# mLSTM tail of a head: denominator and variance products placed one by one behind projection blocks

## What is computed

```
hN = _rmsnorm(x, norm_g[l]);  p = _split_in(hN @ w_in[l])
mq = silu(_causal_dwconv(p["m_q"], ...));  mk = silu(_causal_dwconv(p["m_k"], ...))
s   = einsum('bhld,bhsd->bhls', qc, kc) * exp(logD - m_t[..., None])
num = ... + einsum('bhls,bhse->bhle', s, vc)
den = ... + sum(s, axis=-1)
h   = num / maximum(abs(den), exp(-m_t))[..., None]
var = mean(square(h - mu), axis=-1)
hn  = (h - mu) * rsqrt(var + NORM_EPS)          # times mh_norm_g
ya  = sigmoid(p["m_o"]) * mh * silu(p["m_z"])
```

## Time and profile before

| | us |
|---|---|
| median of three runs | 1608.32 (1608.13 to 1611.36) |
| the profiled execution | 1609.1 |
| its span | 1607.3 |
| TensorE matmuls busy | 1533.4 (95% of the span) |
| VectorE, ScalarE, GpSimd busy | 759.3, 639.4, 684.8 |
| mean granted TensorE clock | 0.983 of full |

### The profile page before, as it was taken

One profiled execution on the slowest core, in us unless ns is written; L12 is line 12 of the kernel. 1 busy time (PEld: TensorE's weight loads), 2 busy tenths in 40 slices (PEclk: granted clock), 3 DMA queues, 4 the chain that ended last, 5 costly groups with the idle time before them and its releaser, 6 DMA issues.

```text
span 1607.3 us, 25456 instructions
## 1 busy us (share of the span) xinstructions
PE 1533.4 (95%) x10002; PEld 1226.4 (76%) x10002; DVE 759.3 (47%) x1767; ACT 639.4 (40%) x1345; POOL 684.8 (43%) x661
## 2 busy tenths in 40 slices
PE   5899999999899899999999899999999989999997
PEld 3777777677688788787877687878788867776887
DVE  4435555455543434534355454733433564455154
ACT  4234444445432533333334353434332344444331
POOL 2534344343432533443435444535255434444462
PEclk8999999999999999999999899999999999999999
DMA  9121111111023322322221322222121221111222
GB/s 395 39 77 42 39 54 53 53 53 54 27 80 105 105 73 79 110 82 80 85 100 53 105 86 79 80 70 88 53 101 57 79 105 53 53 53 53 79 83 75
DMA packets 23143, 128.23 MB, mean 80 GB/s; under 512 B 2417, under 2 KB 4593, under 8 KB 9073
## 3 DMA queue, kind: packets, MB, share of 16 engines
q1 hardware_dynamic: 22880, 126.35, 22.3%
q10 hardware_dynamic: 144, 0.26, 0.0%
HBM read 124.50 MB, written 2.10 MB: 79 GB/s over the span
## 4 chain that ended last, share of the span: by engine, by line
PE 82%; DVE 8%; ACT 3%; issue 3%; POOL 3%; DMA 1%; SPq 0%; POOLq 0%; DVEq 0%; ACTq 0%
PE PS L1516 16%; PE PS L1518 15%; PE PS L1517 15%; PE PS L1596 7%; PE PS L1631 6%; PE PS L1606 6%; PE PS L1509 3%; PE PS L1510 3%; PE PS L1511 3%; DVE sm L2209 2%; PE PS L1684 1%; PE PS L1676 1%; POOL WL L2536 1%; DMA XC<-in_xt 1%; PE PS L1529 1%
## 5 line engine op out<-in xcount | busy, mean ns | idle before, releaser
L2536 POOL TENSOR_TENSOR WL<-W,WH 128x512 fp32r<-128x512 f32 x304 | 400.4, 1332 | 326.7 <-ACT WH L1787 326.5
L1516 PE MATMUL PS<-HX,WH 128*128 128x512 f32 (+1 forms) x1008 | 412.8, 410 | 7.9 <-POOL WL L2536 3.7
L1518 PE MATMUL PS<-HX,WL 128*128 128x512 f32 (+1 forms) x1008 | 391.3, 388 | 0.0
L1517 PE MATMUL PS<-LX,WH 128*128 128x512 f32 (+1 forms) x1008 | 390.7, 388 | 0.0
L1516 PEld LDWEIGHTS PS<-HX,WH 128*128 128x128 f32 x1008 | 193.1, 192 | 54.5 <-issue 14.0
L1518 PEld LDWEIGHTS PS<-HX,WL 128*128 128x128 f32 x1008 | 191.7, 190 | 39.8
L1517 PEld LDWEIGHTS PS<-LX,WH 128*128 128x128 f32 x1008 | 192.7, 191 | 33.3 <-issue 2.6
L1787 ACT CAST WH<-W 128x512 fp32r<-128x512 f32 x320 | 186.9, 619 | 40.9 <-PE PS L1511 21.1
L1873 ACT ACTIVATE AR<-PS,sm 128x768 f32<-128x768 f32 (+4 forms) x160 | 115.5, 722 | 164.1 <-DVE sm L2214 93.7
L2209 DVE TENSOR_REDUCE sm<-PS 128x1 f32<-128x512 f32 (+4 forms) x224 | 150.0, 670 | 51.7 <-PE PS L1596 47.1
L2603 POOL TENSOR_SCALAR AR<-AR,sm 128x768 f32<-128x768 f32 (+1 forms) x96 | 74.8, 779 | 186.9 <-DVE sm L2225 186.9
(11 more groups left out here) (286 smaller groups left out, 2542.7 us busy)
## 6 DMA issues: line engine op xcount, KB each, us to landing
W<-in_wu SPq DMA_DIRECT2D x98, 1024.0 KB, 4.9
AR<-in_wu SPq DMA_DIRECT2D x8, 1024.0 KB, 10.8
AR<-in_biasb SPq DMA_DIRECT2D x32, 256.0 KB, 2.6
XX<-in_xt SPq DMA_DIRECT2D x2, 1024.0 KB, 6.0
XC<-in_xt SPq DMA_DIRECT2D x1, 1024.0 KB, 14.4
out<-XX SPq DMA_DIRECT2D x2, 512.0 KB, 4.1
out<-XX SPq DMA_DIRECT2D x4, 256.0 KB, 2.2
C<-in_cc SPq DMA_DIRECT2D x1, 770.5 KB, 8.4
```

The source lines that it names most:

```text
L1516: e.matmul(o, wh, xh, start=(k == 0), stop=False)
L1517: e.matmul(o, wh, xl, start=False, stop=False)
L1518: t = e.matmul(o, wl, xh, start=False, stop=(k == 7))
L2536: e.tensor_tensor(WL[:, d, a:z], W[:, n % 2, a:z], WH[:, d, a:z].bitcast(F32), ALU.subtract).then_inc(*s_wl_pool.by(n, q))
```

## The change

The two rows `m_den` and `m_var` are cut into single products, `m_den_part` (ten) and `m_var_part` (eight). The whole tail of a head becomes a generator, `m_tail`, and `with_tail` runs a projection and takes one step of the generator behind each of its blocks. It is used for the next head's `mq`, `mk` and `mv` (64 blocks in all), and for `nq` after the last head. Counted in blocks, the denominator's products stand behind blocks 1 to 10, the other engines' `m_den` and the first variance product behind block 11, the last variance product behind block 18, `m_var` of the other engines behind 19, `m_scale` behind 27 (the third block of the second half of `mk`), `parts_y` behind 43. The banks of the ring are taken at these places too. The table steps stay where they were.

```diff
+        def with_tail(g):
+            for _ in g:
+                next(tail[0], None)
...
-                run(pj(g, un, 0, T, 128 * m, "h", o))
+                with_tail(pj(g, un, 0, T, 128 * m, "h", o))
...
-            if later:
-                later.pop(0)()
...
+        def m_tail(hd):
+
             mps["den", hd] = bank(ONE.take(("mden", hd), (s_dsq, (hd,))))
+            for q in range(4):
+                for j in range(q + 1):
+                    do("m_den_part", hd, q, j)
+                    yield
             do("m_den", hd)
-
-        def m_var(hd):
             mps["var", hd] = bank(ONE.take(("mvar", hd), (s_vv, (hd,))))
+            for q in range(4):
+                for m in range(2):
+                    do("m_var_part", hd, q, m)
+                    yield
             do("m_var", hd)
+            for _ in range(8):
+                yield
+            m_scale(hd)
+            for _ in range(16):
+                yield
+            parts_y(hd)
...
-                run(pjt(("mv", hd, s), un, s, "h", o))
+                with_tail(pjt(("mv", hd, s), un, s, "h", o))
...
-            later[:] = [lambda hd=hd: m_den(hd), lambda hd=hd: m_var(hd), lambda hd=hd: m_scale(hd), lambda hd=hd: parts_y(hd)]
+            tail[0] = m_tail(hd)
...
-                run(pj(("nq", m), un, 0, T, 128 * (m % 2), "h", o))
+                with_tail(pj(("nq", m), un, 0, T, 128 * (m % 2), "h", o))
                 do("n_query", m)
                 do_later(3)
+                if m == 3:
+                    run(tail[0])
...
+            def m_den_part(hd, q, j):
+                if q == 0:
+                    free(w, ("mden", hd))
+                t = e.matmul(mps["den", hd][:, q:q + 1], E[j][:, 128 * q:128 * q + 128], c("ones", 0, 1), start=(j == 0), stop=(j == q))
+                if q == 3 and j == 3:
+                    t.then_inc(*s_den.by(hd))
+
+            def m_var_part(hd, q, m):
+                if q == 0 and m == 0:
+                    free(w, ("mvar", hd))
+                    w.wait_ge(*s_nsq(hd, 1))
+                t = e.matmul(mps["var", hd][:, q:q + 1], sqv[m][:, 128 * q:128 * q + 128], c("ones", 0, 1), start=(m == 0), stop=(m == 1))
+                if q == 3 and m == 1:
+                    t.then_inc(*s_vsum.by(hd))
```

More of the change, by code:

```diff
@@ L1185, in conv @@
             un.done(s_proj, *g)
-        later, tabs = [], list(range(1, 6))
+        tail, tabs = [iter(())], list(range(1, 6))
         do("table", 0)
@@ L1192, in do_later @@
                 do("table", tabs.pop(0))
-            if later:
-                later.pop(0)()
-        def m_den(hd):
+        def m_tail(hd):
             mps["den", hd] = bank(ONE.take(("mden", hd), (s_dsq, (hd,))))
+            for q in range(4):
+                for j in range(q + 1):
+                    do("m_den_part", hd, q, j)
+                    yield
             do("m_den", hd)
-        def m_var(hd):
             mps["var", hd] = bank(ONE.take(("mvar", hd), (s_vv, (hd,))))
+            for q in range(4):
+                for m in range(2):
+                    do("m_var_part", hd, q, m)
+                    yield
             do("m_var", hd)
+            for _ in range(8):
[4 more added lines that the diff above has]
+            parts_y(hd)
         def parts_y(hd):
@@ L1685, in m_num @@
                 t.then_inc(*s_hn.by(hd, m))
-            def m_den(hd):
-                free(w, ("mden", hd))
-                o = mps["den", hd]
-                for q in range(4):
-                    for j in range(q + 1):
-                        t = e.matmul(o[:, q:q + 1], E[j][:, 128 * q:128 * q + 128], c("ones", 0, 1), start=(j == 0), stop=(j == q))
-                t.then_inc(*s_den.by(hd))
-            def m_var(hd):
-                free(w, ("mvar", hd))
-                w.wait_ge(*s_nsq(hd, 1))
-                o = mps["var", hd]
-                for q in range(4):
-                    for m in range(2):
-                        t = e.matmul(o[:, q:q + 1], sqv[m][:, 128 * q:128 * q + 128], c("ones", 0, 1), start=(m == 0), stop=(m == 1))
-                t.then_inc(*s_vsum.by(hd))
+            def m_den_part(hd, q, j):
[11 more added lines that the diff above has]
+                    t.then_inc(*s_vsum.by(hd))
             def m_scale(hd):
@@ L1772, in tensor @@
                                score=score, turn=turn, pv=pv, m_gates=m_gates, m_gate_col=m_gate_col, m_exp=m_exp, m_qk=m_qk,
-                               m_num=m_num, m_den=m_den, m_var=m_var, m_scale=m_scale, n_rotate=n_rotate, n_hidden=n_hidden,
+                               m_num=m_num, m_den_part=m_den_part, m_var_part=m_var_part, m_scale=m_scale, n_rotate=n_rotate, n_hidden=n_hidden,
                                n_cmp_out=n_cmp_out, cmp=cmp, cmp_turn=cmp_turn, x_wb=x_wb))
```

## The result

| | before | after |
|---|---|---|
| median, four runs each | 1609.1 us (1608.13 to 1611.36) | 1624.64 us (1624.19 to 1627.87) |
| the profiled execution, its span | 1609.1, 1607.3 | 1624.86, 1623.1 |
| TensorE matmuls busy | 1533.4 | 1534.1 |
| mean granted TensorE clock | 0.983 | 0.982 |

The ratio after to before is 1.0105, with an interval of 1.0091 to 1.0119: slower by about 1%, 16 us. The forecast was 1617.3 us, in a range of 1608.5 to 1621: the direction was right, the size was half, and the range missed the time.

A forecast was written before the change was run, and what follows sets the result against it. TensorE's stream, busy all the time in the heads, was taken as the bound. Waits 11.3, removed drops -4.8, steady -0.3 and new drops +2.8 gave +9.0 us: span 1616.3, time 1617.3 us, range 1608.5 to 1621.

The forecast's parts named there:

- waits in the value projections (with the factor row's): TensorE waits for late value quarters and at the factor row: 3.3, 4.7 and 3.3 us in heads 1 to 3.
- clock drops in the query stretch, gone: Three half-clock stretches behind denominator rows disappear with single placing: 3 x 1.6 = 4.8 us less.
- pairs against rows: On TensorE, 18 pairs at 0.22 us replace rows of 4.04 us a head: 0.3 us less over four heads.
- new drops in the value projections: Half clock after head 2's wait and one other, about 1.4 us each: 2.8 us more.
- The chain on VectorE and GpSimd: Key convolution, `m_scale` multiplications, then value splits: quarter 2 ready at 30.8 us, quarter 3 at 32.1 from head start.
- The table step of head 2: Table load and sine on ScalarE delay the key's copy from 20.5 to 22.0: 1.4 us more wait.
- rival (d): Weight loads of pairs hide behind blocks: one of two, 1609.4 us, chance 0.04; both, 1601.5 us, chance 0.03.
- rival (a): Same value-projection waits, but no clock drop behind them: 1614.5 us; chance 0.17.
- (e): The clock still drops in the query stretch: +4.8 us, 1622.1 us with the forecast's waits; chance 0.03.
- (b): Value-projection waits half as long, 5.6 instead of 11.3 us, without drops: 1608.8 us; chance 0.10.
- (c): GpSimd gets value quarters in time, leaving only gains of 4.8 + 0.3 us: 1603.2 us; chance 0.08.
- Nothing else waits: Beyond the value waits, later gate weights, loads and banks are in time; no further cost, gate weights covered by 4 us.

The follow-up runs named there:

- The filled wait: The changed kernel with 24 extra 256-column matmuls in heads 1 to 3 ahead of the first value tile; 1623.23 us, ratio 1.0089.
- the tail in its old places: The changed kernel with `m_scale` and `parts_y` back between the projections, only the 18 products still placed singly; 1610.77 us, ratio 1.0008.

## Why the prediction was wrong in size

| term, us | predicted | measured |
|---|---|---|
| waits in the value projections (with the factor row's) | +11.3 | +13.3 |
| clock drops in the query stretch, gone | -4.8 | -4.8 |
| pairs against rows | -0.3 | +1.2 |
| new drops in the value projections | +2.8 | +6.4 |
| sum | +9.0 | +16.1 |

The last measured term is what the value projections hold beyond the waits shown (1.75 + 2.84 + 1.78). The filled wait showed that only about half of this is net: 1.65 of 2.84 us in head 2 and 0.84 of 1.78 in head 3; for head 1 an estimate of 1.0 us, from the 2.0 us at half clock that are left after quarter 3 was taken up at 1031.48 (to 1033.5). That makes 3.5 us, near the 2.8 predicted, and leaves 13.3 + 6.4 - 3.5 = 16.2 us for waits where 11.3 stood. So the step that failed is the time at which GpSimd delivers quarter 3: TensorE started the block that needs it 34.8, 34.8 and 34.2 us after the head's start in heads 1 to 3, where the prediction had 32.1, 33.5 and 32.1.

**The chain on VectorE and GpSimd** was right in each of its links and too short in nearly all. In head 3, counted from 1150.95: the copy could start at 20.7 (predicted 20.3), the convolution was done at 27.1 (26.1), GpSimd started the multiplications at 27.8 (26.9) and ended them at 30.7 (29.5), quarter 2 was ready at 32.5 (30.8) and quarter 3 at 34.2 (32.1). The prediction took its durations from the earlier trace rows, where the other engine had been quiet or only partly busy. But the change is what makes the two run at once. VectorE's three multiply-adds took 2.33 us with GpSimd idle, 3.44 beside quarters 0 and 1, 4.44 beside `m_scale` and quarters 2 and 3; a split took 1.7 us beside the last of these, where the earlier trace rows have 1.29. Moving the power behind the splits gave 2.33 again: shown by experiment, for that link; for the other links only the overlap is seen in the rows. The Trainium skill (GPSIMD Engine Reference, 1. Specifications) says that GpSimd shares its SBUF interfaces with VectorE, with contention against VectorE instructions that have two SBUF inputs; the traces agree as far as VectorE's durations go. By that rule those of the earlier trace rows were not to be added up without a margin.

**The table step of head 2** came as predicted (the copy at 1095.33), and the longest single wait is in head 2.

**The pairs** cost 0.235 us each instead of 0.22. TensorE in the first query block, kernel after: from 999.25 to 1000.17 are 0.92 us, a block (0.68) and a pair.

```profile
999.25 0.28 PE L1707 MATMUL PS<-C,AR 128*128 128x1 f32 x2
999.39 0.48 PE L1533 MATMUL PS<-HX,WH 128*128 128x512 f32 x1
999.71 0.39 PE L1534 MATMUL PS<-LX,WH 128*128 128x512 f32 x1
...
1000.17 0.28 PE L1707 MATMUL PS<-C,AR 128*128 128x1 f32 x2
```

Of the pair 0.14 us are its own records; the first wide matmul behind it, whose pitch is 0.32 us (999.39 to 999.71) instead of 0.23, carries the rest. 72 pairs at 0.015 us more are 1.1 of the 1.5 us by which this term was off. The reading by which the loads hide (rival (d)) is out. It rested on the Trainium skill (TensorE: Matmul & The Clock Gate, Part 2, Step-by-step), where weight loads are pulled ahead of matmuls in flight; the trace disagrees with it as far as it was stretched to both loads of a pair.

**The clock.** The step that the three old drops would go held in the trace. But its reason, one row and hence a drop, was too simple: with the rows kept, but six blocks earlier, two of the three old drops went too, and so did, in the trace of the kernel after, the drop behind the 2.40 us wait that the prediction had as its second example. The new drops came in all three heads, and in head 2 twice as long, where two were forecast; rival (a), without drops, is out, and (e) too.

**The rivals of the waits.** (b), half as long, is out. (c), that the quarters come in time, did not happen; more important is that its price was wrong. It said that then only 4.8 + 0.3 us of gain are left. The kernel with the tail in its old places is that case, nearly, and its ratio was 1.0008. "Nothing else waits" had been worked out for what was moved, and not for what was removed: the variance row, and the denominator row with its drop, had covered the chain from the key's first half to quarter 2, with 2.2 us to spare. In the forecast this didn't show, because the larger wait contains it.

**The range** was too narrow for a sum of such terms: three of its four were off to the same side, and the largest rests on a chain of seven durations, each of which was taken from rows in which the other engine had little to do, so that their errors added up.

**What stays open.** Why a drop follows some rows of one-column records and not others, and why drops stand at 1222, 1290 or 1300 in six of the runs (the whole `m_scale` or GpSimd's part late, the cut row, the denominator alone in pairs, the power late, the table step moved) and in none of the other traces; no run was made on it, and how much of this would differ between two executions of one kernel isn't known. The price of head 1's new drop, which stayed in the kernel with the filled wait, is an estimate.

## What to carry to other kernels

When an item of several engines is moved, look at its place in each engine's list, and at what is queued behind it there: TensorE's and VectorE's parts of `m_scale` moved at no cost that shows, and two multiplications on GpSimd, which stood waiting with the next weights behind them, cost 16.9 us of span. When work is removed from the engine that bounds, ask which chain elsewhere it had been covering, and how much room that chain had. And price work that will newly overlap on VectorE and GpSimd by rows in which both are busy. Drops of the clock seen in one trace are best counted over the mean clock of several runs before they enter a sum.

## What was not expected of the hardware

VectorE and GpSimd cost each other more than the rows of before had shown. Three multiply-adds of 128x512 on VectorE: 2.33 us alone, 3.44 and 4.44 beside GpSimd. GpSimd's split of 128x512 took 1.27 us alone and, in head 3, beside the first key convolution; beside that of head 1 the second of two took 1.74, and beside the second key convolution they took 1.7. What makes that difference was not tried. The trace of the kernel before had a warning, outside the rows read from it: the same VectorE op on 128x4 elements with GpSimd idle and beside GpSimd's splits, and these splits.

```profile
1017.10 0.16 DVE L2408 TENSOR_TENSOR sm<-sm 128x4 f32<-128x4 f32 x1
...
1156.48 1.24 DVE L2408 TENSOR_TENSOR sm<-sm 128x4 f32<-128x4 f32 x1
1157.76 1.22 DVE L2410 TENSOR_SCALAR sm<-sm 128x4 f32<-128x4 f32 x1
```

```profile
1156.41 2.54 POOL L2536 TENSOR_TENSOR WL<-W,WH 128x512 fp32r<-128x512 f32 x2 [3.44 <-ACT WH L1787]
```

The two small ops end at 1157.72 and 1158.98, each just behind the end of one of the two splits (1157.7 and 1158.95), and the splits took their usual 2.54 us. So here VectorE alone paid, and what it paid was the length of the other engine's instruction, not a share of its own.

And 20 records of one column, in which the profile shows TensorE busy without a pause, can be followed by 3.4 us at half clock: in one trace of each kernel, three times out of four in the kernel before, once in four in the kernel that has them six blocks earlier, and never in these places for pairs or for a row cut in 12 and 8.
